# Two unused gaps in SBUF that give the mixer inputs' split parts the same offset modulo 512 bytes as the weights' split parts

## What is computed

```python
def first_block(x, c, ...):
    mod = silu(c) @ w_ada + b_ada                      # 6 x 1024 shifts, scales, gates
    h = modulate(rmsnorm(x, norm_mix_g), sh_m, sc_m)
    q, k, v, f_logit, u = split(h @ w_in)              # the mixer
    mix = concat(forgetting_attention(q, k, v, log_f), multiscale_pool(u)) @ w_out
    x = x + gt_m * mix
    h = modulate(rmsnorm(x, norm_ffn_g), sh_f, sc_f)
    x = x + gt_f * hierarchical_moe(h)                 # 32 experts, 2 per token
    return rmsnorm(x, norm_final_g)

def second_block(h, ...):
    u = rmsnorm(h) @ w_in_2                            # 1024 -> 5632
    merged = g_a * (stick_breaking_attention(...) @ w_o_sb) + g_b * (hgrn2(...) @ w_o_hg)
    h = h + merged @ w_out_2
    h = h + square(relu(rmsnorm(h) @ w_ff1)) @ w_ff2   # 1024 -> 4096 -> 1024
    return rmsnorm(h, final_g)
```

## Time and profile before

| what | value |
|---|---|
| median of 3 executions | 766.76 us (766.27 to 768.11) |
| the profiled execution, its own time | 766.49 us |
| its span in the profile | 764.7 us |
| mean granted TensorE clock | 0.965 of full |
| PE busy | 690.5 us, 90% |
| DVE, ACT, POOL busy | 357.0, 295.3, 46.5 us |
| moved by DMA | 210.27 MB, mean 275 GB/s |

### The profile page before, as it was taken

One profiled execution on the slowest core, in us unless ns is written; L12 is line 12 of the kernel. 1 busy time (PEld: TensorE's weight loads), 2 busy tenths in 40 slices (PEclk: granted clock), 3 DMA queues, 4 the chain that ended last, 5 costly groups with the idle time before them and its releaser, 6 DMA issues. The chain is left out here.

```text
span 764.7 us, 13034 instructions
## 1 busy us (share of the span) xinstructions
PE 690.5 (90%) x5466; PEld 538.0 (70%) x5466; DVE 357.0 (47%) x570; ACT 295.3 (39%) x432; POOL 46.5 (6%) x84
## 2 busy tenths in 40 slices
PE   3999999899768577668999999999999999999996
PEld 3887778753323132223999989999889999998895
DVE  3568861421110010104956787435776744565443
ACT  4244430241111010005765553767456543354532
POOL 0000000000000000000065660000000000000000
PEclk9999999999998788989999999999999999999999
DMA  8999899999999999999855334412645445554001
GB/s 354 402 416 405 316 425 419 423 410 423 423 422 423 425 421 424 417 414 421 316 218 194 138 112 137 174 35 102 217 166 193 162 169 220 220 218 168 1 1 55
DMA packets 33039, 210.27 MB, mean 275 GB/s; under 512 B 4689, under 2 KB 5073, under 8 KB 8657
## 3 DMA queue, kind: packets, MB, share of 16 engines
q1 hardware_dynamic: 32976, 209.38, 68.8%
HBM read 208.32 MB, written 1.05 MB: 274 GB/s over the span
## 5 line engine op out<-in xcount | busy, mean ns | idle before, releaser
L419 PE MATMUL psum<-XH,whi 128*128 128x256 f32 x736 | 210.6, 286 | 3.7 <-DVE XL L665 2.6
L419 PE MATMUL psum<-XH,wlo 128*128 128x256 f32 x736 | 208.3, 283 | 0.0
L419 PE MATMUL psum<-XL,whi 128*128 128x256 f32 x736 | 207.9, 282 | 0.0
L512 DVE TENSOR_TENSOR wlo<-raw,whi 128x2048 fp32r<-128x2048 f32 (+1 forms) x88 | 169.0, 1957 | 50.7 <-ACT whi L495 50.7
L495 ACT ACTIVATE whi<-raw 128x2048 fp32r<-128x2048 f32 (+1 forms) x79 | 139.5, 1801 | 40.1 <-PE psum L419 22.4
L419 PEld LDWEIGHTS psum<-XH,whi 128*128 128x128 f32 x736 | 139.1, 189 | 7.5 <-DVE XL L665 3.1
L419 PEld LDWEIGHTS psum<-XL,whi 128*128 128x128 f32 x736 | 138.8, 189 | 0.3
L419 PEld LDWEIGHTS psum<-XH,wlo 128*128 128x128 f32 x736 | 138.9, 189 | 0.0
L419 PE MATMUL psum<-raw,G 128*32 128x512 f32 x456 | 69.2, 694 | 18.7 <-DMA raw<-in_w_exp 18.6
L419 PEld LDWEIGHTS psum<-raw,G 128*32 128x32 f32 x456 | 17.9, 124 | 56.5 <-issue 55.8
L1267 ACT ACTIVATE WT<-psum 128x256 f32<-128x256 f32 x8 | 3.1, 384 | 132.8 <-PE psum L419 98.8
(11 more groups left out here) (349 smaller groups left out, 948.8 us busy)
## 6 DMA issues: line engine op xcount, KB each, us to landing
raw<-in_w_exp SPq DMA_DIRECT2D x85, 1024.0 KB, 22.4
raw<-in_w_ff SPq DMA_DIRECT2D x32, 1024.0 KB, 5.0
raw<-in_w_in SPq DMA_DIRECT2D x22, 1024.0 KB, 5.3
raw<-in_w_ada SPq DMA_DIRECT2D x16, 1024.0 KB, 11.8
raw<-in_w_in_t SPq DMA_DIRECT2D x8, 1024.0 KB, 18.2
X<-in_w_exp SPq DMA_DIRECT2D x5, 1024.0 KB, 24.7
raw<-in_w_ada_q SPq DMA_DIRECT2D x4, 1024.0 KB, 17.4
raw<-in_w_out_t SPq DMA_DIRECT2D x4, 1024.0 KB, 9.8
```

What stands on the lines that cost most here:

```text
L419: return e.matmul(o, l, r, start=start, stop=stop, skip_group_check=True)
L512: e.tensor_tensor(wlo[j % NS][:, x], ring[slot[i]][:, x], whi[j % NS][:, x], ALU.subtract).then_inc(*steps_(("lo", j, x.start // 1024), *[ ...
```

## The change

Two tensors that nothing reads or writes are declared in `build`. `gap0` has 384 bytes a partition and moves all that is declared behind `cst`; `gap1` has 128 bytes and moves all that belongs to one stage by 128 bytes more, 512 in all. The diff is complete:

```diff
--- before.py
+++ after.py
@@ -131,6 +131,7 @@
         for name, n in CONSTS:
             C[name] = cst[:, o_:o_ + n]
             o_ += n
+        sb("gap0", [128, 96])
         X = sb("X", [128, 2, 1024])
         GT = sb("GT", [128, 2048])
         GTM, GTF = GT[:, 0:1024], GT[:, 1024:2048]
@@ -157,6 +158,7 @@
         wgt = sb("wgt", [128, 2, 2])
 
 
+        sb("gap1", [128, 32])
         p1 = ExitStack()
         t1 = tensors(p1)
         xn = t1("xn", [128, 2, 1024])
```

## The result

The changed kernel takes 768.76 us in the median of 15 executions (767.98 to 770.06), the kernel before beside it 766.79 us (766.27 to 768.11). The ratio is 1.0027, with a 95% interval from 1.0019 to 1.0035: 1.5 to 2.7 us slower. I had forecast 767.0 us, a loss of 0.3, with a range from 764.6 to 769.0. The time lies in the range and on the forecast side of 0.3%, but the loss is several times the one that I summed up, and the interval shuts out 0.3 us. So some 1.7 us have another source.

The account below looks back on a forecast made before the run. DMA was taken to bound the kernel to 355 us, PE after. -0.53 us (512 columns) + 0.9 us (256 columns) + 0 for the rest made +0.4 us, so 767.0 us, range 764.6 to 769.0.

Parts of the forecast that it names:

- What bounds the kernel: Whole span: DMA bringing the experts' weights sets the pace to 355 us, PE for the 400 us after.
- The 512-column form: 96 token-major matmuls with XH/XL after 355 us: 226.6 ns instead of 232.1 at distance 0, 0.53 us gained.
- The third rival: All matmuls: the 5.5 ns belong to buffer or time, not distance; nothing changes, 766.8 us; chance 12%.
- The 256-column form: 1,824 matmuls after 355 us: all at 120.0 ns; about 700 slow from 118.6, ff unchanged; 0.9 us lost.
- a short end piece: Kernel's last product, whi/wlo streamed against FH/FL at distance 0: 22 distances of 120.0 ns, taken as the future pace.
- a few `SS` matmuls: Experts' stage, short runs with XNH/XNL at distance 0: ten matmuls at 120.0 ns, taken as the future pace.
- the faster: 256-column matmuls after 355 us gain 5.5 ns each too, 10.0 us in all, 756.8 us; chance 7%.
- the slower rival: 256-column matmuls after 355 us settle above 120.0 ns, at 122.5 for example, 5.7 us lost, 772.4 us; chance 5%.
- The PE sum of +0.4 us: Matmuls after 355 us: 0.53 us gained with 512 columns, 0.9 us lost with 256 columns, nothing else.
- Transfers: Experts' weights, 145 to 355 us, into moved X, raw15, raw16: rate 410 to 425 GB/s whichever the target, price 0.
- Everything before 355 us: 384 256-column matmuls lose 0.54 us, 96 512-column ones gain 0.53, the DMA stream hides part: 0.
- the upper bound of 769.0: Whole kernel: 512-column gain fails, 256-column loss, mixer's 0.5 and small 0.3 come in full: 768.6, plus 0.4 spread.

Follow-up runs that it names:

- 256 and 64 apart: Against the kernel before, XH put 256 bytes, XL 64, MH 32 and ML 256 from the weights' parts modulo 512; one execution, 766.65 us.
- Parts only: Against the kernel before, only XH, XL and XT moved, to 128 modulo 512; run twice: 767.60 us (1.0006) and 767.52 us (1.0003).
- The targets alone: Against the kernel before, X, GT, raw15 and raw16 moved to 128 modulo 512, XH, XL and XT kept at 256; 768.46 us, 1.0018.
- all at 256 or 0: Changed kernel with everything from raw0 on shifted, so all starts are 256 or 0 modulo 512; 766.17 and again 765.93 us (256), 766.52 us (0).

## Why the prediction was right, and where it was not

**What bounds the kernel.** Right: DMA to 355 us, PE behind it, both before and after. In the experiments the targets moved the 55 transfers and not PE's part, the distance PE's part and not the transfers.

**The 512-column form.** Right in kind, nearly in size. Forecast 226.6 ns for 232.1; measured 227.3 in the first block, that is 0.23 of the 0.26 us that it was to give. The third rival (nothing depends on the distance) fell with it, and with it the reading of the Trainium skill's rule ("SBUF — State Buffer", Who interferes with whom) that two independent read ports rule out any such dependence. `XH` kept its instructions and its neighbours, and changed its pace when its distance did, from 232.1 to 227.3 ns. The rule may hold for the ports; it doesn't hold for the time.

**The 256-column form.** Right: 120.0 ns in the long run where 118.6 stood, 11.51 us for 96 in ff as before. That a short end piece and a few `SS` matmuls could stand for 1,824 others held. The reason I added, that the loading of the next block sets 120 and nothing is left to win, was argued and is refuted by the 117.7 ns at 256 and 64 apart: 120 isn't a floor. Neither the faster nor the slower rival came, though the former was right that this form could still become faster, at another distance.

**The PE sum of +0.4 us.** Parts only gave +0.5 and +0.2 us by the ratios, each about 0.7 uncertain. The profiles say more: from the hybrid's start to the end, 0 apart takes 400.6 us and 128 apart 400.1 to 400.2, or 400.5 in the profile of before. Right.

**Transfers.** This is the step that failed: "each slice of the page from the 9th to the 18th shows 410 to 425 GB/s whichever is the target: 0". The targets alone cost 1.4 us (0.8 to 2.1), more than three times the PE sum, and that made most of the change's 2 us. The slices can't carry that sentence. A slice of 19 us holds seven or eight transfers to all kinds of targets, and the effect is 1% of the rate, 26 ns in 2,485, while the slices differ among themselves by 3%. The trace of before held the answer: grouped by target, 4% slow packets stand against 54%. I compared buffers by their distance modulo 512 for PE and DVE, and never asked for their own start for DMA. The Trainium skill ("DMA: Bandwidth & Descriptors", How a descriptor splits into AXI transactions) has the rule that I should have weighed: a descriptor is split in pieces of 256 bytes that start at multiples of 256, so one that starts off such a boundary needs a piece more. The runs agree with its boundary (256 as good as 0, and 128, 160 and 192 alike in time), while the price that they show is 1.2% of the rate (426 against 421 GB/s). Counted as the page's table counts, in beats of 32 bytes, an 8 KB packet that starts 128 off needs 260 for 256, which as an estimate is 1.6%; by whole pieces it would be 33 for 32, 3%. Its text speaks of reads; here it was the side that writes to SBUF that moved.

**Everything before 355 us.** For PE's terms neither shown nor refuted. The hybrid of the two parts-only kernels began at 364.66 and 365.04 us in their profiles, 0.5 and 0.8 later than before, but two executions of one program differed by 3.1 there. What I didn't see is that the DMA stream that hides PE's terms is itself where a slower transfer shows in full.

**Chances.** I gave 0.87 to a result within 0.3% and 0.06 to a slower one. It came out at 0.27% slower, near that border, on a side for which I had named only PE's mechanism; the mechanism that moved it was priced at nothing. That 768.76 us lies under the upper bound of 769.0 is luck: the bound had been built from PE terms at their worst, and the transfers filled that room.

## What to carry to other kernels

An unused gap is an edit to everything behind it: before pricing it, list every buffer that moves, and for each its start (for DMA) and its distance from the operands it is read with (for PE), because the two are different questions with different answers. In a stretch that DMA sets, let each large target begin at a multiple of 256 bytes; here one declaration was worth about 3 us of 767 against the changed kernel, and 1 to 1.4 against the one before. And an effect of 1% is not bounded by a view whose own rows differ by 3%: group the packets by target first, and compare a length between two events within the stretch, which here agreed to 0.1 us where spans scattered by 3.

## What the runs showed of the hardware that I had not expected

- An 8 KB packet into SBUF takes 309 ns where the target begins at a multiple of 256 bytes (94 to 95% of them in the kernels with all at 256 or 0), and often 311 to 322 ns at 128, 160 or 192; the rate is 426 against 421 GB/s.
- The two transfers that follow three well-placed targets in the ring are fast too, though they begin at 128 (2% slow packets, 69% once the three have moved).
- PE's pace in a back-to-back stream of `float32r` matmuls depends on the distance modulo 512 of streamed and loaded operand: 512 columns 226.6 to 227.5 ns at 0, 232.1 at 128, 231 to 232 with 256 mixed with 64 or 32; 256 columns 120.0 at 0, 118.6 or 120.0 at 128, 117.7 with 256 and 64 mixed.
- The granted clock around 155 us differs from one execution of the same program to the next, 1.00 or 0.75, and the hybrid's start by 3.1 us; about half of that had arisen by 165 us.
